# The first mixer's transposes, norms and output projection in another order

## The chip, the cores and the metric

The kernel runs on one core of one Trainium2 chip. The time is the device time of one execution in microseconds (us). Before the change it is 2455.3 us, the median of 3 runs (2453.57 to 2457.45).

## What is computed

256 tokens of width 1024 in float32 go through two blocks of two layers each. A layer of the first block, where the change lies, is a mixer and a gated feed-forward part:

```python
h = _rms_norm(x, attn_norm[l]) @ w_in[l]      # latent q, latent kv, rope key, differential q, k, v, grouped q, k, v
q_a  = (_rms_norm(h_cq) @ mla_w_uq[l])        # 6 latent heads, q and k normed and rotated
kv_a = (_rms_norm(h_ckv) @ mla_w_ukv[l])
o_a = softmax(q_a k_a) v_a
o_b = rms_norm((softmax(q1 k1) - lam * softmax(q2 k2)) v_b) * (1 - lambda_init)   # 4 differential heads
o_c = softmax(q_c k_c) v_c                    # 6 grouped heads on 2 key heads, rotated along two axes
x = x + concat(o_a, o_b, o_c) @ w_o[l]
x = x + (silu(xn @ gate) * (xn @ up)) @ w_down[l]
```

The second block (two other mixers, a dense and a mixture-of-experts feed-forward part) is not touched.

## The kernel before

**Weights.** Every float32 product is made of three: operands are split into a rounded part (hi) and the rest (lo), and `mm3` (lines 484 to 486) issues hi x hi, hi x lo and lo x hi. Weights come as a stream of halves of 128 x 1024, loaded by SP's queue into a ring of 8, cast by ACT (`w_hi`, line 420) and subtracted by DVE or, for the halves in `pool_halves` (the grouped chunks and eight of the ten halves of the output projection), by POOL (`w_lo`, line 426) into rings of 4. Each `half_step` makes PE use one half while ACT and DVE or POOL prepare the one three ahead.

**Units.** Activations that serve as an operand are transposed by PE in a unit (`unit`, line 673): up to four transposes into one bank (line 686), ACT copies hi (lines 691, 694), DVE subtracts lo (lines 699, 702). With `lag=1` PE waits until all units so far have their lo part; with `lag=2` one may be open.

**Ahead of the attention.** `first_layer` computes w_in's columns in chunks of two to four halves (`chunk`, `gemm_cols`): latent q, latent kv, differential q (2), differential k (3), then the products of the normed latents (`latent_rows`, query with three halves, key/value with two), then differential v (4). Each is evacuated by ACT and DVE (lines 994, 999, 1029, 1031). Beside the halves stand callbacks: beside chunk 2 the squares, three transposed units of the latents (`latent_blocks`) and a transposed gain (`gain_column`), beside chunk 3 the norm and rotation of the differential queries in three parts (`rotate`: squares and their sums, rotation, scaling), then their two units (`diff_blocks`); beside the query product the rotation of the keys, beside chunk 4 their units.

**The attention.** `attention` (line 709) is a pipeline over 20 maps (8 differential, 6 latent, 6 grouped), written out for each engine in program order; each engine has its own in-order queue, and semaphores alone tie them. In step s PE computes map s's scores; DVE takes their maximum (lines 780, 782), ACT the exponentials (line 792). PE transposes the probabilities of map s-2 (line 807), ACT copies them (line 733); PE multiplies those of map s-3 with the values (line 829), and DVE scales and writes the output (lines 835 to 846). Then comes `aside`, the filler `fill(step)` (line 1269), and behind it `units(step)` (line 1228):

- the filler holds PE's halves of the grouped chunks (`column_halves`) in steps 0 to 11 and, from step 15, one half of the output projection a step (`out_half`, 12 products of 512 columns into banks 4 to 7), the last two behind the loop; and DVE's norms and rotations of the latent heads (steps 0 to 5, lines 1098 to 1122), of the grouped queries (7 to 9) and keys (11, 12), and the norm of the differential outputs (`diff_norm`, lines 1157 to 1171, steps 11 and 12);
- units: the latent heads' in steps 6 to 11, the grouped ones in 12 and 13, behind them two units of the differential outputs, and from step 15 on, every second step, those of the other outputs. All those up to step 13 have `lag=1`.

DVE's part of a unit stands in its queue behind DVE's filler of the same step, PE's behind PE's.

Of the kernel before, what the change touches and what calls it, by code (L numbers as in the profile page):

```python
# [242 lines left out]
def build(nc, A):  # L243
    ctx = ExitStack()
    with ctx:
# [463 lines left out]
        def attention(E, maps, aside, act_copies=False, units=None, lag=1):  # L709
# [28 lines left out]
            if E.kind == "pe" and "made" not in maps[0]:  # L738

                e.wait_ge(qk_lo, E.qk.at())  # L740

                wait(e, acc_act, values)
                wait(e, acc_dve, values)
            for step in range(M + lag + 1):
# [69 lines left out]
                if 0 <= m < M:  # L814
# [17 lines left out]
                    if E.kind == "dve":  # L832
# [43 lines left out]
        def first_layer(E, l):  # L876
# [80 lines left out]
            def latent_blocks():  # L957


                if E.kind == "pe":  # L960
                    e.wait_ge(tp_lo, E.tp.at())
                    e.wait_ge(acc_act, E.acc.at())
                    e.wait_ge(acc_dve, E.acc.at())
                places = [(pair_of(b_cq), 0, 2), (pair_of(b_cq + 2, 1), 2, 1),
                          ((x_hi[:, KD:KD + nk, :], x_lo[:, KD:KD + nk, :]), nq, nk)]
                for dst, j, n in places:
                    g = CG_Q + j
                    unit(E, 2 + E.qk.n % 2, dst, [blk(H, C_CQ + (j + i) * P) for i in range(n)],
                         gains=colg[:, l, g:g + n], lag=2)

            def diff_blocks(c, b0):

                if E.kind == "pe":
                    e.wait_ge(qk_src, E.qks.at())
                for j in range(0, DH, 2):
                    unit(E, 2 + E.qk.n % 2, pair_of(b0 + j), [blk(H, c + (j + i) * P) for i in range(2)], lag=2)
# [69 lines left out]
            def beside_dk(hx):  # L1046
                if hx < 3:
                    rotate(hx, C_DQ, F_DQ, at_q)

            def beside_uq(hx):  # L1050
                rotate(hx, C_DK, F_DK, at_k)

            def beside_dv(hx):
                if hx == 2:
                    if E.kind == "pe":

                        e.wait_ge(acc_act, E.acc.at())
                        e.wait_ge(acc_dve, E.acc.at())
                    diff_blocks(C_DK, DH)
# [6 lines left out]
            chunk(2, beside_dq)  # L1066
            chunk(3, beside_dk)
# [4 lines left out]
            latent_rows(nk, MH * (MNOPE + MV) // 2, 0, (x_hi[:, KD:KD + nk, :], x_lo[:, KD:KD + nk, :]), KV, at_l + 2,  # L1072
                        nothing)
            chunk(4, beside_dv)

# [81 lines left out]
            def diff_norm(part):  # L1157

                x = O[:, :, MH * MV:MH * MV + DH * DV].rearrange("p t (h d) -> p t h d", h=DH)
                y = sc_mla[:, 0:TB * DH * DV]  # L1160
                if part == 0:
                    if E.kind == "dve":
                        drain_dve(E)
                        head_squares(E, x, DH, DV, 0, y)
                        mean_ready(E, 0, TB * DH, DV)
                    rsqrt(E, 0, TB * DH)
                elif E.kind == "dve":
                    need_rs(E)
                    e.tensor_tensor(x, x, scales(0, DH, DV), ALU.mult).then_inc(qk_src, 1)
# [58 lines left out]
            def units(step, ask=False):  # L1228
# [4 lines left out]
                if 6 <= step < 6 + MH:  # L1233
# [6 lines left out]
                    bk = 6 if step < 8 else 4 + step % 2  # L1240
                    unit(E, bk, pair_of(place(2 * h), 2, MQK), [blk(QA, h * MQK, MQK), blk(KA, h * MQK, MQK)], w=MQK)
                    ready[h] = E.qk.at()
                if step == 12 or step == 13:
# [3 lines left out]
                    unit(E, 4 + step % 2, pair_of(b_gq + j), [blk(H, C_GQ + (j + i) * P) for i in range(2)])  # L1247
# [47 lines left out]
            for h in range(DH):  # L1295
                for c in range(2):
                    o = MH * MV + h * DV
                    maps.append(dict(q=(h, c * 64, c * 64 + 64), k=(DH + h, c * 64, c * 64 + 64),
                                     scale=DQ ** -0.5, width=DV, minus=c == 1, ready=lambda n=E.qk.at(): n,
# [15 lines left out]
            for n in (8, 9):  # L1315
                out_half(n)
# [1292 lines left out]
```

## Time and profile before

| what | value |
|---|---|
| median of 3 runs | 2455.3 us |
| profiled execution | 2458.2 us |
| its span on the core | 2456.3 us |
| PE busy | 2310.7 us (94%) |
| DVE busy | 1733.9 us (71%) |
| ACT busy | 1460.9 us (59%) |
| POOL busy | 238.4 us (10%) |
| mean granted clock of TensorE | 0.968 |

The profile is of one execution. A clock of 1.00 is TensorE's full 2.4 GHz, 0.50 is 1.2 GHz; a mean between them is a share of time at each. The mixer of layer 0 lies between some 24 and 226 us of the span, that of layer 1 between some 430 and 625.

### The profile page before, as it was taken

The numbers are of one execution on the slowest core, as the hardware profiler recorded it, in microseconds if no ns is written. First come the engines' busy times: TensorE is split into PE (matmuls) and PEld (weight loads), VectorE is DVE, ScalarE is ACT, GpSimd is POOL, SyncE is SP. The second block draws the span as 40 slices with busy tenths as digits, with TensorE's granted clock in tenths as the row PEclk, the third lists the DMA queues.
The fourth block names the chain that finished last, engine by engine and source line by source line (L and its number), as shares of the span: only waits on it lengthen the run. The fifth ranks groups of instructions, "written<-read, shape, count | busy, mean of one in ns | idle before, by whom it ended". The sixth has DMA issues, their size and how long they took to land.

```text
span 2456.3 us, 31647 instructions
## 1 busy us (share of the span) xinstructions
PE 2310.7 (94%) x11904; PEld 1964.2 (80%) x11904; DVE 1733.9 (71%) x2370; ACT 1460.9 (59%) x2105; POOL 238.4 (10%) x140
## 2 busy tenths in 40 slices
PE   5889999888999899899899979999999999999997
PEld 5777887777788799788789868888888888888885
DVE  5864555773555544655653669989899999999998
ACT  4444444444444456444445557777777777777776
POOL 0422000142000232100215000000000000000000
PEclk9979999998999999999999989999999999999998
DMA  7313554521555544455463449999999999999996
GB/s 251 123 41 133 194 189 156 186 81 56 176 189 188 179 138 128 159 194 188 145 204 127 131 172 357 354 357 357 353 361 355 360 350 363 343 370 343 368 343 238
DMA packets 156989, 570.92 MB, mean 232 GB/s; under 512 B 18528, under 2 KB 18880, under 8 KB 156192
## 3 DMA queue, kind: packets, MB, share of 16 engines
q1 hardware_dynamic: 153744, 555.58, 64.6%
q0 software_dynamic: 3088, 13.27, 1.5%
q8 instruction: 97, 1.59, 0.2%
q14 instruction: 60, 0.49, 0.1%
HBM read 567.72 MB, written 1.05 MB: 232 GB/s over the span
## 4 chain that ended last, share of the span: by engine, by line
PE 86%; DVE 8%; ACT 2%; DMA 1%; issue 1%; POOL 1%; SPq 0%; DVEq 0%; POOLq 0%; ACTq 0%
PE bank L484 24%; PE bank L486 23%; PE bank L485 23%; PE bank L1729 3%; PE bank L1730 2%; PE bank L1731 2%; PE bank L829 2%; PE bank L1385 2%; PE bank L2199 1%; PE bank L807 1%; DVE w_lo L426 1%; PE bank L2220 1%; DMA arena<-in_bgate 1%; PE bank L686 1%; DVE X L1624 1%
## 5 line engine op out<-in xcount | busy, mean ns | idle before, releaser
L426 DVE TENSOR_TENSOR w_lo<-raw,w_hi 128x1024 fp32r<-128x1024 f32 x986 | 1192.2, 1227 | 320.1 <-ACT w_hi L420 292.2
L420 ACT CAST w_hi<-raw 128x1024 fp32r<-128x1024 f32 x1055 | 1101.4, 1051 | 364.7 <-PE bank L486 306.9
L484 PE MATMUL bank<-w_hi,x_hi 128*128 128x512 f32 (+2 forms) x2592 | 1024.5, 395 | 28.3 <-POOL w_lo L426 6.0
L486 PE MATMUL bank<-w_hi,x_lo 128*128 128x512 f32 (+2 forms) x2592 | 1004.2, 387 | 0.0
L485 PE MATMUL bank<-w_lo,x_hi 128*128 128x512 f32 (+2 forms) x2592 | 1002.7, 387 | 0.0
L484 PEld LDWEIGHTS bank<-w_hi,x_hi 128*128 128x128 f32 x2592 | 493.3, 190 | 123.4 <-POOL w_lo L426 9.5
L486 PEld LDWEIGHTS bank<-w_hi,x_lo 128*128 128x128 f32 x2592 | 491.8, 190 | 98.8
L485 PEld LDWEIGHTS bank<-w_lo,x_hi 128*128 128x128 f32 x2592 | 493.4, 190 | 89.8
L426 POOL TENSOR_TENSOR w_lo<-raw,w_hi 128x1024 fp32r<-128x1024 f32 x69 | 166.9, 2426 | 387.4 <-ACT w_hi L420 387.2
L1606 POOL TENSOR_TENSOR small<-small 128x1 f32<-128x1 f32 x10 | 8.6, 862 | 1353.9 <-ACT small L1602 1353.9
L1729 PE MATMUL bank<-x_hi,w_hi 128*128 128x256 f32 x384 | 111.6, 291 | 0.0
L1730 PE MATMUL bank<-x_lo,w_hi 128*128 128x256 f32 x384 | 109.1, 284 | 0.0
L1731 PE MATMUL bank<-x_hi,w_lo 128*128 128x256 f32 x384 | 109.1, 284 | 0.0
L1391 ACT CAST x_hi<-bank 128x256 fp32r<-128x256 f32 x112 | 41.9, 374 | 81.8 <-PE bank L2199 43.5
L829 PE MATMUL bank<-arena,PT 128*128 128x64 f32 (+1 forms) x576 | 81.3, 289 | 6.6 <-DVE O L846 6.0
L829 PEld LDWEIGHTS bank<-arena,PT 128*128 128x128 f32 x576 | 77.8, 210 | 8.1 <-issue 8.1
L733 ACT COPY PT<-bank 128x512 f32<-128x512 f32 x56 | 32.8, 586 | 77.6 <-PE bank L807 77.6
L1410 ACT ACTIVATE arena<-bank 128x256 f32<-128x256 f32 x134 | 50.4, 384 | 44.0 <-PE bank L486 44.0
L1730 PEld LDWEIGHTS bank<-x_lo,w_hi 128*128 128x128 f32 x384 | 74.2, 193 | 0.0
L1729 PEld LDWEIGHTS bank<-x_hi,w_hi 128*128 128x128 f32 x384 | 74.2, 193 | 0.1
L1731 PEld LDWEIGHTS bank<-x_hi,w_lo 128*128 128x128 f32 x384 | 74.0, 193 | 0.0
L792 ACT ACTIVATE PP<-bank,small 128x256 f32<-128x256 f32 x80 | 37.3, 473 | 56.2 <-DVE small L782 56.0
(226 smaller groups left out, 1869.1 us busy)
## 6 DMA issues: line engine op xcount, KB each, us to landing
raw<-in_stream SPq DMA_DIRECT2D x1055, 512.0 KB, 5.7
tab<-in_lngb POOLq DMA_DIRECT2D x5, 1024.0 KB, 7.9
arena<-in_rpb POOLq DMA_DIRECT2D x16, 256.0 KB, 7.4
tab<-in_rowv POOLq DMA_DIRECT2D x2, 640.0 KB, 8.1
X<-in_x SPq DMA_DIRECT2D x1, 1024.0 KB, 5.2
out_y<-X SPq DMA_DIRECT2D x2, 512.0 KB, 2.6
tab<-in_ropec POOLq DMA_DIRECT2D x2, 448.0 KB, 5.1
tab<-in_ropes POOLq DMA_DIRECT2D x2, 448.0 KB, 6.2
```

Source lines behind the costliest of these rows:

```text
L420: nc.scalar.copy(w_hi[:, s % SPLIT, :], raw[:, slot, :]).then_inc(hi_done, 1)
L426: e.tensor_tensor(w_lo[:, s % SPLIT, :], raw[:, s % RAW, :], w_hi[:, s % SPLIT, :].bitcast(F32), ALU.subtract).then_inc(done, 1)
L484: pe.matmul(out, xh, wh, start=first, stop=False)
L485: pe.matmul(out, xh, wl, start=False, stop=False)
L486: return pe.matmul(out, xl, wh, start=False, stop=last)
L829: i = e.matmul(ob[:, tb * w:(tb + 1) * w], PT[:, m % 2, kb, tb * P:(tb + 1) * P], a["v"](kb), start=kb == 0, stop=kb == TB - 1)
L1385: i = e.transpose(tr[f][:, tb * P:(tb + 1) * P], HH[:, tb, f * P:(f + 1) * P], ident[:, :])
L1391: i = nc.scalar.copy(hT_hi[:, :, 0:T], both)
L1410: i = nc.scalar.activation(SIL[:, tb, :], bank[b0 + tb][:, 0:FC], ACT.Silu, scale=rsx[:, tb:tb + 1] if scaled else 1.0)
L1729: e.matmul(out, wh, xh, start=first, stop=False, skip_group_check=True)
L1730: e.matmul(out, wh, xl, start=False, stop=False, skip_group_check=True)
L1731: return e.matmul(out, wl, xh, start=False, stop=last, skip_group_check=True)
```

## The change

Units now stand ahead of the step's filler on every engine, except those of steps 15, 17, 19 and 21, which stay behind it. All units up to step 13 have `lag=2`, and the first two take two banks. The norm of the differential outputs is made in two halves of two heads: the first in steps 6 and 7, the second in 10 and 11; its first unit moves from step 13 to 11. The grouped key chunk's second half moves from step 10 to 9. The output projection starts in step 14, and one half instead of two is left behind the loop. Ahead of the attention, the three latent units stand behind halves 1, 2 and 3 of chunk 2, the gain column beside chunk 3; the rotation of the differential keys is spread over the query product's second half and both halves of the key/value product; the four differential units stand beside and behind chunk 4, a query and a key unit in turn. The two waits in front of the attention's first step go; the one for the evacuation stands ahead of the first filler half.

```diff
--- before.py
+++ after.py
@@ attention
-            if E.kind == "pe" and "made" not in maps[0]:
-                e.wait_ge(qk_lo, E.qk.at())
-                wait(e, acc_act, values)
-                wait(e, acc_dve, values)
...
+                if units and not units(step, True):
+                    units(step)
                 aside(step)
-                if units:
-                    if E.kind == "pe" and lag <= step < M + lag and units(step, True):
+                if units and units(step, True):
+                    if E.kind == "pe" and step < M + lag:
                         e.wait_ge(*copied(step - lag))
                     units(step)
@@ ahead of the attention
-            def latent_blocks():
-                if E.kind == "pe":
+            def latent_blocks(which):
+                if E.kind == "pe" and which == 0:
...
-                for dst, j, n in places:
-                    g = CG_Q + j
-                    unit(E, 2 + E.qk.n % 2, dst, ..., gains=colg[:, l, g:g + n], lag=2)
+                dst, j, n = places[which]
+                g = CG_Q + j
+                unit(E, 2 + which % 2, dst, ..., gains=colg[:, l, g:g + n], lag=2)
-            def diff_blocks(c, b0):
+            def diff_blocks(j, q):
+                c, b0 = (C_DQ, 0) if q else (C_DK, DH)
                 if E.kind == "pe":
-                    e.wait_ge(qk_src, E.qks.at())
-                for j in range(0, DH, 2):
-                    unit(E, 2 + E.qk.n % 2, pair_of(b0 + j), ..., lag=2)
+                    e.wait_ge(qk_src, diff_made[q])
+                unit(E, 3 if q else 2, pair_of(b0 + j), ..., lag=2)
+                diff_ready[j // 2] = E.qk.at()
             def beside_dq(hx):
                 if hx == 0:
                     latent_squares()
-                if hx == 1:
-                    latent_blocks()
-                if hx == 2:
-                    gain_column()
+                else:
+                    latent_blocks(hx - 1)
             def beside_dk(hx):
+                if hx == 0:
+                    gain_column()
                 if hx < 3:
                     rotate(hx, C_DQ, F_DQ, at_q)
+                if hx == 2:
+                    diff_made[1] = E.qks.at()
             def beside_uq(hx):
-                rotate(hx, C_DK, F_DK, at_k)
+                if hx == 1:
+                    rotate(0, C_DK, F_DK, at_k)
+            def beside_ukv(hx):
+                rotate(hx + 1, C_DK, F_DK, at_k)
+                if hx == 1:
+                    diff_made[0] = E.qks.at()
             def beside_dv(hx):
-                if hx == 2:
-                    if E.kind == "pe":
-                        e.wait_ge(acc_act, E.acc.at())
-                        e.wait_ge(acc_dve, E.acc.at())
-                    diff_blocks(C_DK, DH)
+                if hx == 1 and E.kind == "pe":
+                    e.wait_ge(acc_act, E.acc.at())
+                    e.wait_ge(acc_dve, E.acc.at())
+                if hx:
+                    diff_blocks(hx // 3 * 2, hx % 2)
...
             chunk(3, beside_dk)
-            diff_blocks(C_DQ, 0)
             latent_rows(nq, ..., at_l, beside_uq)
...
-            latent_rows(nk, ..., at_l + 2, nothing)
+            latent_rows(nk, ..., at_l + 2, beside_ukv)
             chunk(4, beside_dv)
+            diff_blocks(2, 0)
@@ diff_norm
-            def diff_norm(part):
-                x = O[:, :, MH * MV:MH * MV + DH * DV]...
+            def diff_norm(h0, part):
+                n = DH // 2
+                at = h0 * TB
+                x = O[:, :, MH * MV + h0 * DV:MH * MV + (h0 + n) * DV]...
@@ units
-                    bk = 6 if step < 8 else 4 + step % 2
-                    unit(E, bk, pair_of(place(2 * h), 2, MQK), ..., w=MQK)
+                    bk = 6 + step % 2 if step < 8 else 4 + step % 2
+                    unit(E, bk, pair_of(place(2 * h), 2, MQK), ..., w=MQK, lag=2)
                     ready[h] = E.qk.at()
+                if step == 11:
+                    if E.kind in ("act", "dve"):
+                        e.wait_ge(og_done, l + 1)
+                    if E.kind == "pe":
+                        e.wait_ge(qk_src, made["diff01"])
+                        e.wait_ge(acc_act, E.acc.at())
+                        e.wait_ge(acc_dve, E.acc.at())
+                    out_unit(6, 3, 2, 2 * DH, scale=og_col[:, 0:1], lag=2)
                 if step == 12 or step == 13:
...
-                    unit(E, 4 + step % 2, pair_of(b_gq + j), ...)
+                    unit(E, 4 + step % 2, pair_of(b_gq + j), ..., lag=2)
                 if step == 13:
-                    if E.kind in ("act", "dve"):
-                        e.wait_ge(og_done, l + 1)
                     if E.kind == "pe":
-                        e.wait_ge(qk_src, made["diff"])
-                        e.wait_ge(acc_act, E.acc.at())
-                        e.wait_ge(acc_dve, E.acc.at())
-                    for j in range(2):
-                        out_unit(6 + j, 3 + 2 * j, 2, 2 * DH, scale=og_col[:, 0:1])
+                        e.wait_ge(qk_src, made["diff23"])
+                    out_unit(7, 5, 2, 2 * DH, scale=og_col[:, 0:1], lag=2)
@@ fill
                 if step in (0, 2, 4, 6, 7):
+                    if step == 0 and E.kind == "pe":
+                        wait(e, acc_act, E.acc.at())
+                        wait(e, acc_dve, E.acc.at())
                     next(gq, None)
-                if step in (8, 10, 11):
+                if step in (8, 9, 10):
                     if step == 8 and E.kind == "pe":
-                        e.wait_ge(qk_lo, E.qk.at())
+                        e.wait_ge(qk_lo, ready[1])
                     next(gkv, None)
-                if step >= 15:
-                    out_half(step - 15)
+                if step >= 14:
+                    out_half(step - 14)
...
+                if step == 6:
+                    diff_norm(0, 0)
+                if step == 7:
+                    diff_norm(0, 1)
+                    made["diff01"] = E.qks.at()
...
+                if step == 10:
+                    diff_norm(DH // 2, 0)
                 if step == 11:
-                    diff_norm(0)
+                    diff_norm(DH // 2, 1)
+                    made["diff23"] = E.qks.at()
                     grouped(0, C_GK, GKV, F_GK, at_g + TB * GH)
                 if step == 12:
-                    diff_norm(1)
-                    made["diff"] = E.qks.at()
...
             out_unit(2, 9, 1, 0)
-            for n in (8, 9):
-                out_half(n)
+            out_half(9)
```

## Rows read from the trace of the kernel before

**Rows 1.** The page: busy time by engine, and the chain that ended last.

```profile
PE 2310.7 (94%) x11904; PEld 1964.2 (80%) x11904; DVE 1733.9 (71%) x2370; ACT 1460.9 (59%) x2105; POOL 238.4 (10%) x140
...
PE 86%; DVE 8%; ACT 2%; DMA 1%; issue 1%; POOL 1%; SPq 0%; DVEq 0%; POOLq 0%; ACTq 0%
```

**Rows 2.** Busy us by stretch, layer 0: PE, PEld, DVE, ACT, POOL; clock.

```profile
66.70:84.20 17.50, 11.73 (x68) 11.17 (x68) 16.70 (x20) 9.58 (x13) 2.90 (x1) 0.90 0.42 136
...
99.90:124.40 24.50, 20.10 (x122) 17.84 (x123) 23.58 (x43) 11.44 (x32) 11.47 (x4) 0.89 0.26 85
...
124.40:169.80 45.40, 34.22 (x231) 32.17 (x230) 33.31 (x73) 20.57 (x53) 12.46 (x6) 0.80 0.11 36
...
169.80:182.60 12.80, 12.80 (x53) 11.26 (x52) 3.19 (x9) 4.64 (x12) 2.38 (x1) 0.58 0.01 1
...
182.60:226.40 43.80, 39.66 (x222) 32.56 (x220) 15.71 (x35) 17.91 (x36) 9.53 (x4) 1.00 0.35 111
```

**Rows 3.** The same view, second layer.

```profile
522.70:568.30 45.60, 33.19 (x227) 31.35 (x226) 33.27 (x73) 20.54 (x53) 12.46 (x6) 0.84 0.12 37
...
568.30:581.50 13.20, 13.20 (x53) 11.56 (x52) 3.19 (x9) 4.64 (x12) 2.37 (x1) 0.56 0.02 4
```

**Rows 4.** PE timeline ahead of the attention: start, us, [idle before, releaser].

```profile
49.54 0.65 PE L686 MATMUL bank<-ident,arena 128*128 128x128 f32 x4 [1.63 <-DVE qk_l L702]
...
68.66 1.09 PE L686 MATMUL bank<-ident,arena 128*128 128x128 f32 x8 [1.99 <-DVE arena L942]
...
71.65 0.61 PE L484 MATMUL bank<-w_hi,qk_t 128*128 128x288 f32 x1 [1.90 <-DVE qk_l L699]
...
84.25 0.47 PE L484 MATMUL bank<-w_hi,x_hi 128*128 128x512 f32 x1 [1.96 <-DVE arena L1031]
...
98.94 0.35 PE L484 MATMUL bank<-qk_t 64*128 64x256 f32 x1 [1.05 <-DVE arena L999]
```

**Rows 5.** DVE's timeline ahead of the attention and at its first step.

```profile
69.66 0.74 DVE L999 TENSOR_SCALAR arena<-bank,small 128x512 f32<-128x512 f32 x1
...
86.33 1.13 DVE L1031 TENSOR_SCALAR arena<-bank,small 128x384 f32<-128x384 f32 x2
...
99.92 0.69 DVE L780 TENSOR_REDUCE small<-bank 128x2 f32<-128x512 f32 x1 [1.23 <-PE bank L486]
```

**Rows 6.** DVE's timeline in the attention's steps 3 to 13.

```profile
112.58 3.22 DVE L1108 TENSOR_TENSOR arena<-arena,small 128x1152 f32<-128x1152 f32 x1
...
128.81 0.69 DVE L699 SCALAR_TENSOR_TENSOR qk_l<-bank,qk_t 96x512 fp32r<-96x512 f32 x1 [2.25 <-ACT qk_t L691]
...
137.49 3.34 DVE L665 TENSOR_TENSOR arena<-arena,tab 128x192 f32<-128x192 f32 x4
...
150.91 0.69 DVE L699 SCALAR_TENSOR_TENSOR qk_l<-bank,qk_t 96x512 fp32r<-96x512 f32 x1 [2.98 <-ACT qk_t L691]
...
153.24 1.23 DVE L650 TENSOR_TENSOR arena<-O 128x1024 f32<-128x1024 f32 x1
...
165.06 0.69 DVE L699 SCALAR_TENSOR_TENSOR qk_l<-bank,qk_t 128x512 fp32r<-128x512 f32 x1 [1.18 <-ACT qk_t L691]
...
170.62 0.75 DVE L699 SCALAR_TENSOR_TENSOR x_lo<-bank,small,x_hi 128x512 fp32r<-128x512 f32 x1 [1.99 <-ACT x_hi L691]
```

**Rows 7.** POOL's timeline, two of its weight splits in the attention.

```profile
112.24 2.35 POOL L426 TENSOR_TENSOR w_lo<-raw,w_hi 128x1024 fp32r<-128x1024 f32 x1
...
137.53 2.55 POOL L426 TENSOR_TENSOR w_lo<-raw,w_hi 128x1024 fp32r<-128x1024 f32 x1 [1.11 <-ACT w_hi L420]
```

**Rows 8.** PE's timeline, steps 14, 15, 20 and 21 of the attention.

```profile
169.79 0.58 PE L484 MATMUL bank<-qk_t 64*128 64x256 f32 x1
...
178.06 0.77 PE L484 MATMUL bank<-w_hi,x_hi 128*128 128x512 f32 x1
...
206.85 0.48 PE L484 MATMUL bank<-w_hi,x_hi 128*128 128x512 f32 x1
...
209.71 0.60 PE L807 MATMUL bank<-ident,PP 128*128 128x128 f32 x4
```

More of the change, by code:

```diff
@@ L965, in latent_blocks @@
                           ((x_hi[:, KD:KD + nk, :], x_lo[:, KD:KD + nk, :]), nq, nk)]
-                for dst, j, n in places:
-                    g = CG_Q + j
-                    unit(E, 2 + E.qk.n % 2, dst, [blk(H, C_CQ + (j + i) * P) for i in range(n)],
-                         gains=colg[:, l, g:g + n], lag=2)
-            def diff_blocks(c, b0):
+                dst, j, n = places[which]
+                g = CG_Q + j
+                unit(E, 2 + which % 2, dst, [blk(H, C_CQ + (j + i) * P) for i in range(n)],
+                     gains=colg[:, l, g:g + n], lag=2)
+            def diff_blocks(j, q):
+                c, b0 = (C_DQ, 0) if q else (C_DK, DH)
                 if E.kind == "pe":
-                    e.wait_ge(qk_src, E.qks.at())
-                for j in range(0, DH, 2):
-                    unit(E, 2 + E.qk.n % 2, pair_of(b0 + j), [blk(H, c + (j + i) * P) for i in range(2)], lag=2)
+                    e.wait_ge(qk_src, diff_made[q])
+                unit(E, 3 if q else 2, pair_of(b0 + j), [blk(H, c + (j + i) * P) for i in range(2)], lag=2)
+                diff_ready[j // 2] = E.qk.at()
             def gain_column():
@@ L1072, in first_layer @@
             latent_rows(nk, MH * (MNOPE + MV) // 2, 0, (x_hi[:, KD:KD + nk, :], x_lo[:, KD:KD + nk, :]), KV, at_l + 2,
-                        nothing)
+                        beside_ukv)
             chunk(4, beside_dv)
+            diff_blocks(2, 0)
             def place(n):
@@ L1163, in diff_norm @@
                         drain_dve(E)
-                        head_squares(E, x, DH, DV, 0, y)
-                        mean_ready(E, 0, TB * DH, DV)
-                    rsqrt(E, 0, TB * DH)
+                        head_squares(E, x, n, DV, at, y)
+                        mean_ready(E, at, TB * n, DV)
+                    rsqrt(E, at, TB * n)
                 elif E.kind == "dve":
                     need_rs(E)
-                    e.tensor_tensor(x, x, scales(0, DH, DV), ALU.mult).then_inc(qk_src, 1)
+                    e.tensor_tensor(x, x, scales(at, n, DV), ALU.mult).then_inc(qk_src, 1)
                 if part == 1:
@@ L1239, in units @@
                             e.wait_ge(acc_dve, E.acc.at())
-                    bk = 6 if step < 8 else 4 + step % 2
-                    unit(E, bk, pair_of(place(2 * h), 2, MQK), [blk(QA, h * MQK, MQK), blk(KA, h * MQK, MQK)], w=MQK)
+                    bk = 6 + step % 2 if step < 8 else 4 + step % 2
+                    unit(E, bk, pair_of(place(2 * h), 2, MQK), [blk(QA, h * MQK, MQK), blk(KA, h * MQK, MQK)], w=MQK,
+                         lag=2)
                     ready[h] = E.qk.at()
+                if step == 11:
[6 more added lines that the diff above has]
+                    out_unit(6, 3, 2, 2 * DH, scale=og_col[:, 0:1], lag=2)
                 if step == 12 or step == 13:
@@ L1246, in units @@
                         e.wait_ge(qk_src, made["gq" if j == 0 else "gk"])
-                    unit(E, 4 + step % 2, pair_of(b_gq + j), [blk(H, C_GQ + (j + i) * P) for i in range(2)])
+                    unit(E, 4 + step % 2, pair_of(b_gq + j), [blk(H, C_GQ + (j + i) * P) for i in range(2)], lag=2)
                     ready[MH] = E.qk.at()
                 if step == 13:
-                    if E.kind in ("act", "dve"):
-                        e.wait_ge(og_done, l + 1)
                     if E.kind == "pe":
-                        e.wait_ge(qk_src, made["diff"])
-                        e.wait_ge(acc_act, E.acc.at())
-                        e.wait_ge(acc_dve, E.acc.at())
-                    for j in range(2):
-                        out_unit(6 + j, 3 + 2 * j, 2, 2 * DH, scale=og_col[:, 0:1])
+                        e.wait_ge(qk_src, made["diff23"])
+                    out_unit(7, 5, 2, 2 * DH, scale=og_col[:, 0:1], lag=2)
                 if step == 15:
@@ L1298, in first_layer @@
                     maps.append(dict(q=(h, c * 64, c * 64 + 64), k=(DH + h, c * 64, c * 64 + 64),
-                                     scale=DQ ** -0.5, width=DV, minus=c == 1, ready=lambda n=E.qk.at(): n,
+                                     scale=DQ ** -0.5, width=DV, minus=c == 1, ready=lambda h=h: diff_ready[h // 2],
                                      v=lambda kb, h=h: H[:, kb, C_DV + h * DV:C_DV + (h + 1) * DV],
```

7 lines of the change are left out of this document (4 added, 3 removed).

## The prediction

> **What bounds the kernel now.** I read the page first, for the shares of the span; then the busy time in stretches of the mixer; then the timelines of PE and DVE, for who waits for whom. On the page PE is busy 94% of the span and carries 86% of the chain that ended last, DVE 8% [rows 1]. The change touches only the first block's mixer, twice (layers 0 and 1), so the averages do not price it. The stretches do. Between 124.4 and 169.8 us (steps 6 to 13 of the attention) PE is busy 34.22 of 45.40 us at a mean clock of 0.80; in steps 14 and 15 it is busy all 12.80 us, but at 0.58; after that 39.66 of 43.80 at 1.00 [rows 2]. Layer 1 repeats it within a few tenths: 33.19 of 45.60, then 13.20 at 0.56 [rows 3]. So everything below is worked out on layer 0 and doubled. Steps 0 to 5 are DVE's: 23.58 of 24.50 us busy [rows 2], so whatever moves step 0 on DVE moves the rest with it. DMA's share in these stretches is 0.42, 0.26, 0.11, 0.01 and 0.35: SP's weight loads, whose order stays, are no bound here, and the later stages move up with whatever the mixer gives.
>
> **Ahead of the attention.** Three stalls of PE are addressed.
>
> Latent units, one behind each half of the differential-query chunk instead of three in a row: the wait of 1.63 us for the first unit's lo part goes [rows 4]. What is late next is DVE: it must evacuate this chunk and rotate while PE runs the next, and the third unit's lo now stands ahead of that evacuation. Of the 1.6 I pass on 1.1.
>
> Differential-query blocks out of the gap behind the key chunk: today PE waits 1.99, transposes 1.09, waits 1.90 and starts the query product at 71.65 [rows 4]. Without them it still waits for DVE's evacuation of the chunk, which ends at 69.66 + 0.74 = 70.40 [rows 5]: 1.25 gained, not 5.
>
> Key rotation spread over the query and the key/value products: DVE evacuates the query product before two of the three parts instead of behind all, so the wait of 1.96 ahead of the values' chunk goes [rows 4]. In exchange the first differential unit, behind that chunk's second half, waits for the key/value product's evacuation. That ended at 86.33 + 1.13 = 87.46 [rows 5] with no rotation ahead of it; now two parts of the rotation stand there. Replaying DVE's queue with today's durations puts it at about 87.8, against a PE ready at 85.4: a new wait of 2.4. The four units cost as many transposes as before, in smaller groups: 0.1. Less time at the slow clock behind the old gap: I take 0.8 of gain.
>
> At the seam, step 0's scores no longer wait 1.05 for the chunk's evacuation [rows 4], but on DVE that evacuation and two lo parts now stand ahead of step 0's maximum, which started at 99.92 [rows 5]. It comes 3.3 us behind the chunk's end, against 2.0 now: +1.3.
>
> Sum: -1.1 - 1.25 - 1.96 + 2.4 + 0.1 - 0.8 + 1.3 = **-1.3 us**. Bounds 0 (the new wait eats it all) and -3 (it does not occur). It passes whole through steps 0 to 5.
>
> **Steps 6 to 13.** Units now stand ahead of the filler. Today DVE runs the filler while PE, behind its own filler, has yet to transpose; where DVE has no filler it waits: 2.25 in step 6, 2.98 in step 10, then 1.18 and twice about 1.99 in step 13, where four units follow each other one round trip at a time [rows 6]. Sum 10.4. What stays of them: 0.45 in steps 6 and 10, and 1.2 in step 13, where the two output units take other banks and may run one ahead: 2.1.
>
> Added: in steps 7, 8, 9, 11 and 12 DVE now waits in front of its filler, and behind that filler is the next step's maximum, for which ACT's exponentials and PE wait. No row shows this wait in these places. Bounds: 0.5, if DVE's own reciprocal and output work covers it, and 2.98, the longest wait for the same releaser [rows 6]. Nearest is the 1.18 at 165.06, where ACT came straight from the exponentials to the unit, as it will now [rows 6]; part of that lies under the output evacuation of the heads with the minus sign. I take 0.85: 5 x 0.85 = 4.25. The norm in two halves: a 1024-element operation is 1.23 [rows 6], a 512-element one 0.69 [rows 5], so 2 x 0.69 - 1.23 = 0.15 for each of three, and one more small one: 0.6. The second power on POOL is needed only a step later, and covered.
>
> So the last lo comes 10.4 - 2.1 - 4.25 - 0.6 = 3.45 earlier. Step 14's scores, started at 169.79 [rows 8], ran 1.6 ahead of the end of that last lo (170.62 + 0.75 = 171.37 [rows 6]); now they run 0.75 ahead, one unit: 3.45 - 0.85 = 2.6 gained.
>
> Against it stands POOL. L1108 took 3.22 us beside POOL's weight split of 112.24, where 1152 elements at L650's rate are 1.4; the four L665 took 3.34 beside the split of 137.53, where they are some 1.2 [rows 6, 7]: about 2.0 lost each time. The Trainium skill, "SBUF — State Buffer", section "Who interferes with whom", says that a DVE instruction with two SBUF inputs and a GpSimd one that reads SBUF exclude each other, the later blocking until the first is done; the trace agrees. The unit ahead moves ACT's split in step 6, and the key chunk's half moves from step 10 to 9, so two of POOL's splits may newly meet fillers. Bounds 0 and 4.0; I take 1.2, since reductions, units' lo parts and evacuations fill much of that time. Net **-1.4 us**.
>
> **The output projection a step earlier.** A half with the clock up is 209.71 - 206.85 = 2.86 us [rows 8]. It leaves the tail: **-2.9 us**, since the steps after, of PE's, keep one half each, and the waits for the last units are the same. It does not fall into idle time: PE is busy all of steps 14 and 15. But it is at the low level of 1.2 GHz: two steps without a half took 178.06 - 169.79 = 8.3 us, 4.1 each [rows 8]. Now: step 14's attention work slow, 4.1; its half between 2.86 and 5.7, I take 3.9; then step 15 at full clock, 2.1 + 2.9 + 0.6 for its unit: 13.6, against 12.80 [rows 2]. **+0.8 us** (bounds -2.3 and +4.6, below).
>
> **Sum**: -1.3 - 1.4 + 0.8 - 2.9 = -4.8 a layer, -9.6 for both. The profiled execution took 2458.2 us for a span of 2456.3; it would take 2448.6. The median of the runs is 2.9 under it, so **2445.7 us**. Other edits (the waits in front of the attention dropped, bank 7 beside 6, the gain column a chunk later) have no queue behind them that is late.
>
> **Rivals.**
>
> A, the forecast: its own range 2440 to 2451, chance 0.48.
>
> B, the clock comes up with step 14: both steps at full clock are 2 x (2.1 + 2.9) + 0.5 = 10.5, 2.3 under now, 3.1 a layer better than A: **2439.5**. For it: between 169.8 and 182.6 PE was busy throughout and still at 0.58, and the clock rose only behind the first dense half [rows 2, 8]. The page "TensorE: Matmul & The Clock Gate" of the Trainium skill, section "Part 4: PE-mode transpose", says that transposes do not count as PE work for the clock; with a dense half in step 14 that rule favours B. Against: the half itself still starts slow. 0.18.
>
> C, POOL's splits hit fully: 4.0 instead of 1.2, so -2.0 a layer: **2451.3**, within 0.2%. 0.14.
>
> D, slower: DVE's new waits in front of the fillers are as long as today's longest. PE transposes only behind the output product, which waits for DVE's last output, so both could wait in turn. At 2.6 each: 5 x (2.6 - 0.85) = +8.75, +3.95 a layer: **2463.2**. It decides from 2.3 us a wait. Against it: ACT has nothing between exponentials and unit. 0.08.
>
> E, the earlier half does not do what it is moved for: it runs slow to its end and step 15's attention too, 4.1 + 5.7 + 4.1 + 2.9 + 0.6 = 17.4, 3.8 over A's 13.6: -1.0 a layer: **2453.3**. 0.12.
>
> **How the numbers follow.** A measurement of this kernel can tell about 0.2%, 4.9 us, from no change. Faster by more: nearly all of A, B, a sixth of C: 0.70. Within: C, E and A's edge: 0.22. Slower by more: D, 0.08. The range 2437 to 2455 takes in B, C and E and leaves out D and B's far side.
>
> **What would show it.** Right: the seam's maximum on DVE 1 to 2 us earlier; PE's 1.63 and 1.96 gone and a wait of some 2.4 in the values' chunk; waits of DVE for ACT's unit of 0.5 to 1.2 in steps 7 to 13 and none of 2 or more; step 14's scores some 3 us earlier; a half between steps 14 and 15. Wrong: steps 6 to 13 no shorter than 45 us (C, D), or the stretch from step 14 to 16 near 10.5 (B) or 17 (E).

## The result and the profile after

| kernel | median | runs | profiled execution | its span |
|---|---|---|---|---|
| before, measured beside it | 2456.44 us | 10 | 2458.2 us | 2456.3 us |
| after | 2463.47 us | 10 | 2463.08 us | 2461.2 us |

The ratio is 1.0027, with an interval of 1.0017 to 1.0037: slower by 6.6 us by the ratio, by 7.0 by the medians. The forecast was 9.6 us faster, and the time lies above its range. Two executions at a low granted clock, one of the kernel after (2931.45 us, clock 0.744) and one of e8_again below (3731.3 us, clock 0.572, the only profiled one of that run, whose trace is therefore not read), stand in the medians and not in the ratios.

The page of the kernel after, to be read against [rows 1]: PE has the same work, DVE 10 us more, and the chain names DVE and "issue" one per cent more each.

```profile
span 2461.2 us, 31662 instructions
...
PE 2310.2 (94%) x11904; PEld 1960.2 (80%) x11904; DVE 1744.1 (71%) x2378; ACT 1457.0 (59%) x2105; POOL 245.1 (10%) x142
...
PE 85%; DVE 9%; ACT 2%; issue 2%; DMA 1%; POOL 1%; SPq 0%; DVEq 0%; POOLq 0%; ACTq 0%
```

That says only that a wait was added. Where it stands is read from stages. I cut every kernel's mixer at the same events, by their starts on the timelines: the first latent unit on PE; step 0's and step 6's maximum on DVE; the scores of steps 14 and 16 on PE; the first transpose behind the mixer. For the kernel after, layer 0, the view of stretches (PE, PEld, DVE, ACT and POOL busy, granted clock, DMA's share, GB/s) has one row for each stage:

```profile
45.49:103.55 58.06, 46.20 (x216) 39.10 (x215) 40.45 (x45) 22.93 (x32) 17.29 (x6) 0.88 0.44 147
103.55:128.02 24.47, 18.59 (x124) 15.87 (x123) 23.56 (x45) 11.32 (x32) 11.47 (x4) 0.99 0.24 80
128.02:173.06 45.04, 33.95 (x228) 31.20 (x227) 36.95 (x78) 20.22 (x54) 14.14 (x7) 0.84 0.11 36
173.06:186.34 13.28, 13.28 (x65) 11.24 (x65) 2.94 (x9) 4.88 (x12) 3.85 (x2) 0.79 0.14 41
186.34:227.44 41.10, 36.95 (x210) 30.31 (x209) 15.72 (x35) 16.84 (x35) 8.07 (x4) 1.00 0.35 113
```

The lengths of these stages in all kernels, in us, layer 0 / layer 1. The kernels from e1_rs on are those of the experiments, below. All lengths are of one execution each, and the first stage moves by itself by up to 1.5: e5_half has the code of before there, but 52.70 against 51.19 in layer 1, where PE's wait ahead of the values' chunk is 2.00 in the one and 0.66 in the other.

| kernel | ahead of step 0 | steps 0-5 | 6-13 | 14-15 | tail | sum |
|---|---|---|---|---|---|---|
| before | 52.83 / 51.19 | 24.49 / 24.50 | 45.38 / 45.65 | 12.85 / 13.24 | 43.78 / 43.81 | 179.33 / 178.39 |
| after | 58.06 / 58.08 | 24.47 / 24.49 | 45.04 / 45.03 | 13.28 / 14.85 | 41.10 / 41.05 | 181.95 / 183.50 |
| e1_rs | 55.39 / 54.30 | 24.47 / 24.49 | 45.05 / 45.04 | 13.44 / 13.49 | 41.04 / 41.06 | 179.39 / 178.38 |
| e6_dvesplit | 50.57 / 50.56 | 24.50 / 24.48 | 45.05 / 45.07 | 14.26 / 13.57 | 41.07 / 41.08 | 175.45 / 174.76 |
| e2_rot | 50.00 / 51.68 | 24.46 / 24.46 | 45.04 / 45.04 | 13.84 / 13.92 | 41.08 / 41.06 | 174.42 / 176.16 |
| e4_pre | 58.23 / 59.89 | 24.48 / 25.56 | 43.37 / 44.14 | 13.29 / 12.65 | 43.78 / 43.82 | 183.15 / 186.06 |
| e3_attn | 51.72 / 50.13 | 24.50 / 24.47 | 45.03 / 45.02 | 13.15 / 13.75 | 41.06 / 41.04 | 175.46 / 174.41 |
| e5_half | 52.71 / 52.70 | 24.49 / 24.49 | 44.85 / 44.86 | 14.32 / 14.32 | 41.04 / 41.03 | 177.41 / 177.40 |
| e8_seam | 50.34 / 48.83 | 24.52 / 24.50 | 45.05 / 45.07 | 14.25 / 14.35 | 41.08 / 41.08 | 175.24 / 173.83 |
| e9_order | 48.86 / 48.84 | 24.49 / 24.50 | 45.59 / 44.85 | 14.53 / 14.29 | 41.08 / 41.08 | 174.55 / 173.57 |

Of the kernel after one stage is long: ahead of step 0, +5.2 and +6.9. The tail gave its 2.7, and steps 6 to 13, for which most of the change is written, moved by 0.3 and 0.6. The sums of both layers differ by 7.7 us, the two profiled spans by 4.9: the part ahead of layer 0's first latent unit is 1.6 shorter, the part behind layer 1's tail 1.5 shorter and the part between the mixers 0.3 longer. No edit stands there, and the cause was not looked for.

**The long stage.** PE's timeline of the kernel after, with the query product, the first halves of the values' chunk, and its first unit:

```profile
67.87 0.58 PE L484 MATMUL bank<-w_hi,qk_t 128*128 128x288 f32 x1 [4.50 <-DVE arena L996]
...
79.11 0.39 PE L484 MATMUL bank<-w_hi,x_hi 128*128 128x512 f32 x1
...
82.51 0.50 PE L484 MATMUL bank<-w_hi,x_hi 128*128 128x512 f32 x1 [0.47 <-DVE w_lo L426]
...
91.62 1.09 PE L686 MATMUL bank<-ident,arena 128*128 128x128 f32 x4 [6.09 <-issue]
92.36 0.78 PE L484 MATMUL bank<-w_hi,x_hi 128*128 128x512 f32 x1
...
97.23 0.60 PE L686 MATMUL bank<-ident,arena 128*128 128x128 f32 x4
...
100.42 1.03 PE L686 MATMUL bank<-ident,arena 128*128 128x128 f32 x8
```

The query product starts 22.4 us behind the stage's begin, where it was 24.6 (71.65, [rows 4], less 47.09), and the values' chunk 33.6 instead of 37.2. So 3.5 us have been gained by 79.11. Then PE stands still for 6.09 ahead of the first differential unit, and the half behind it takes 4.87 (92.36 to 97.23) where the next takes 2.83 (97.59 to 100.42). The releaser is given as "issue": the profile doesn't name it. By the program it is the evacuation of the key/value product on DVE (L1028), which must end before PE may transpose. DVE's timeline shows it and what stood ahead of it:

```profile
72.25 1.22 DVE L426 TENSOR_TENSOR w_lo<-raw,w_hi 128x1024 fp32r<-128x1024 f32 x1 [3.51 <-ACT w_hi L420]
...
81.23 1.23 DVE L426 TENSOR_TENSOR w_lo<-raw,w_hi 128x1024 fp32r<-128x1024 f32 x1 [3.02 <-ACT w_hi L420]
...
86.08 3.25 DVE L426 TENSOR_TENSOR w_lo<-raw,w_hi 128x1024 fp32r<-128x1024 f32 x1
...
90.39 1.13 DVE L1028 TENSOR_SCALAR arena<-bank,small 128x384 f32<-128x384 f32 x2
...
103.55 0.68 DVE L774 TENSOR_REDUCE small<-bank 128x2 f32<-128x512 f32 x1
```

The evacuation ends at 91.52, and PE goes on at 91.62. Ahead of it DVE waited 3.02 for a cast of ACT's, and one weight split took 3.25 instead of 1.2. ACT's timeline has the cause of the first, POOL's of both:

```profile
75.15 0.89 ACT L1026 ACTIVATE arena<-bank,small 128x288 f32<-128x288 f32 x2 [0.49 <-PE bank L486]
80.14 2.00 ACT L420 CAST w_hi<-raw 128x1024 fp32r<-128x1024 f32 x2 [4.11 <-POOL small L541]
```

```profile
76.31 3.81 POOL L541 TENSOR_TENSOR small<-small 128x16 f32<-128x16 f32 x1 [13.75 <-DVE small L655]
85.06 3.19 POOL L426 TENSOR_TENSOR w_lo<-raw,w_hi 128x1024 fp32r<-128x1024 f32 x1 [4.95 <-ACT w_hi L420]
```

L541 is the power that makes the scales of a norm. The one of 76.31 belongs to the differential keys; ACT needs nothing of it. But `latent_rows` opens on ACT with `need_rs`, which waits until all scales asked for so far are made, and ahead of the key/value product the keys' scales are among them. They were so before the change too, and the count that is waited for is the same. What changed is when they are asked for: beside the query product's first half before, beside its second half now. POOL's and ACT's timelines of the kernel before, at the same place:

```profile
75.55 2.90 POOL L541 TENSOR_TENSOR small<-small 128x16 f32<-128x16 f32 x1 [10.21 <-DVE small L655]
```

```profile
78.16 0.89 ACT L1029 ACTIVATE arena<-bank,small 128x288 f32<-128x288 f32 x2 [0.48 <-PE bank L486]
78.94 1.05 ACT L420 CAST w_hi<-raw 128x1024 fp32r<-128x1024 f32 x1
```

There the power began 3.9 us behind the query product's start (71.65, [rows 4]) and was over at 78.45, while ACT was busy until 79.05 with the evacuation that stands ahead of its wait. So ACT didn't stand, by 0.6 us. In the kernel after, the power begins 8.4 us behind that start (67.87); ACT has done the same evacuation at 76.04 and stands 4.11 us, until 76.31 + 3.81 = 80.12, for scales that it doesn't use. Its casts come late, DVE's splits behind them, and POOL's first split of the grouped weights (85.06 to 88.25) lies beside DVE's of 86.08. **A wait for everything asked for so far grew, because a request that it had always included was moved later**; neither the wait's line nor its count is in the diff. This is the theory that the experiments test. Its rivals are that the new wait is the one forecast (rotation in front of the evacuation), only longer, and that the loss lies in the attention (rival D).

### The profile page after: what moved, and what is told of

It reads as the page before. It is cut to its first block, busy times and chain, and to the rows that moved or that the text cites. A ratio compares the mean times of both kernels' runs of the same rounds, so it can differ in the third digit from the quotient of the medians.

```text
span 2461.2 us, 31662 instructions
## 1 busy us (share of the span) xinstructions
PE 2310.2 (94%) x11904; PEld 1960.2 (80%) x11904; DVE 1744.1 (71%) x2378; ACT 1457.0 (59%) x2105; POOL 245.1 (10%) x142
## 3 DMA queue, kind: packets, MB, share of 16 engines
HBM read 567.72 MB, written 1.05 MB: 231 GB/s over the span
## 4 chain that ended last, share of the span: by engine, by line
PE 85%; DVE 9%; ACT 2%; issue 2%; DMA 1%; POOL 1%; SPq 0%; DVEq 0%; POOLq 0%; ACTq 0%
PE bank L484 24%; PE bank L486 23%; PE bank L485 23%; PE bank L1750 3%; PE bank L1751 2%; PE bank L1752 2%; PE bank L823 2%; PE bank L1406 2%; PE bank L2220 1%; PE bank L801 1%; DVE w_lo L426 1%; PE bank L2241 1%; DMA arena<-in_bgate 1%; DVE small L774 1%; DVE X L1645 1%
## 5 line engine op out<-in xcount | busy, mean ns | idle before, releaser
L823 PEld LDWEIGHTS bank<-arena,PT 128*128 128x128 f32 x576 | 72.8, 198 | 23.6 <-issue 23.6
```

The costliest lines, as they stand in the source:

```text
L823: i = e.matmul(ob[:, tb * w:(tb + 1) * w], PT[:, m % 2, kb, tb * P:(tb + 1) * P], a["v"](kb), start=kb == 0, stop=kb == TB - 1)
```

## The experiments

The times of before are of runs on the same chip beside each kernel; they moved between 2456.4 and 2457.0.

**e1_rs**: ACT waits for the latents' scales alone. Edit to the kernel after:

```diff
                 rsqrt(E, at_l, 4)
+                latent_rs[0] = E.rs.at()
...
                 if E.kind == "act":
-                    need_rs(E)
+                    e.wait_ge(rs_ready, latent_rs[0])
```

> The changed kernel, but ACT waits ahead of each latent product for the latents' own scales (the count right behind their request) instead of for every scale asked for so far. Theory (the wait): in the changed kernel the keys' first rotation part stands ahead of the key/value product, so ACT's wait includes its scales; ACT stood 4.1 us (80.14), DVE 3.0 behind it, a POOL split then met a DVE split (3.25 instead of 1.2). Expected: ACT's 4.1 and DVE's 3.0 gone in both layers, PE's wait in the values' chunk 6.1 down to 3 or less, step 0's maximum 3 to 6.5 us earlier a layer; 6 to 13 us under the changed kernel, so between 2450 and 2457 where the kernel before is 2456 and the changed one 2463. Rival (load): DVE's moved work alone makes the gap; then the wait moves, and the time stays within 2 us of the changed kernel.

Measured: 2457.42 us, ratio to before 1.0005 (0.9996 to 1.0014), 6.0 less than the kernel after. In the trace ACT's 4.11 and DVE's 3.02 are gone. PE's timeline, then DVE's and POOL's, at the same unit:

```profile
89.40 1.08 PE L686 MATMUL bank<-ident,arena 128*128 128x128 f32 x4 [3.40 <-issue]
```

```profile
84.85 3.39 DVE L938 TENSOR_TENSOR arena<-PP,small 128x1024 f32<-128x1024 f32 x1
88.17 1.13 DVE L1031 TENSOR_SCALAR arena<-bank,small 128x384 f32<-128x384 f32 x2
```

```profile
84.50 2.66 POOL L426 TENSOR_TENSOR w_lo<-raw,w_hi 128x1024 fp32r<-128x1024 f32 x1 [3.65 <-ACT w_hi L420]
```

The edit loosens the wait ahead of both latent products, but ahead of the query product ACT didn't stand for POOL in the kernel after. So the wait ahead of the key/value product cost 6.0 us of the execution. That is the small end of the 6 to 13 expected, and PE's wait, 3.40, is above the 3 that was. The kernel is still no faster than before: the last part of the rotation now meets POOL's split, 3.39 for 1.2, and the evacuation is late again, by less.

**e2_rot**: the keys' rotation wholly beside the query product, as before the change; all else as after.

```diff
             def beside_uq(hx):
-                if hx == 1:
-                    rotate(0, C_DK, F_DK, at_k)
-
-            def beside_ukv(hx):
-                rotate(hx + 1, C_DK, F_DK, at_k)
-                if hx == 1:
+                rotate(hx, C_DK, F_DK, at_k)
+                if hx == 2:
                     diff_made[0] = E.qks.at()
```

> The changed kernel with the keys' rotation back beside the three halves of the query product, as before. Theory (the wait): its scales are then asked for a half earlier, and nothing but splits stands ahead of the key/value evacuation: no wait of 4.1 on ACT, none over 1 us in the values' chunk, but the 1.96 for the query product's evacuation is back. Expected 2449 to 2453 (attention's 2.6 a layer kept, 0 to 1.5 a layer gained ahead of it). Rival (load): the four units in the values' chunk and the seam cost by themselves; then 2458 or more.

Measured: 2448.22 us, ratio 0.9964 (0.9950 to 0.9977), 15.2 under the kernel after and 0.8 under the range expected. The stage ahead is 50.00 and 51.68. PE's timeline has the wait that the spreading was to remove, smaller than the 1.96 of [rows 4], and no wait ahead of the first differential unit:

```profile
80.31 0.47 PE L484 MATMUL bank<-w_hi,x_hi 128*128 128x512 f32 x1 [1.16 <-ACT arena L1026]
...
85.85 0.60 PE L686 MATMUL bank<-ident,arena 128*128 128x128 f32 x4
```

**e3_attn and e4_pre**: the change in two, each a version of the kernel before. e3_attn has all edits inside and behind the attention (units ahead of the filler, the norm in halves, the moved key half, the half in step 14, no waits in front of step 0), e4_pre all those ahead of it.

```diff
+                if units and not units(step, True):
+                    units(step)
                 aside(step)
...
-                if step >= 15:
-                    out_half(step - 15)
+                if step >= 14:
+                    out_half(step - 14)
```

> Only the attention's part of the change (units ahead of the filler, norm in halves, output projection from step 14); everything ahead of the attention as before. From the changed kernel's trace: steps 6 to 13 0.35 shorter, steps 14 and 15 0.45 longer, the tail 2.7 shorter, 2.6 a layer: 2451 where the kernel before is 2456 (2449 to 2453). Rival: the attention's part loses by itself (new DVE waits ahead of fillers, and POOL's splits): 2456 or more.

> Only the part ahead of the attention; the attention as before, its two waits in front among it. Both theories: about 5.2 us a layer lost there, less 0 to 1 a layer from the seam, which keeps the old order of waits: 2464 to 2468 where the kernel before is 2456. If it is 2459 or less, the two parts hurt each other and the sum is not of parts.

Measured: e3_attn 2449.21 us, ratio 0.9974 (0.9963 to 0.9985), −7.2; e4_pre 2470.46 us, ratio 1.0057 (1.0044 to 1.0071), +14.1. They add up: 14.1 − 7.2 = 6.9, where the whole change is +7.0. e4_pre is 2.5 above the range expected. The whole loss is ahead of the attention, +5.4 and +8.7 in the table (one other stage of e4_pre, steps 0 to 5 of layer 1, is 1.1 longer than in all others, which was not looked into), and in e4_pre ACT's timeline has the same wait, now 4.95:

```profile
80.89 1.99 ACT L420 CAST w_hi<-raw 128x1024 fp32r<-128x1024 f32 x2 [4.95 <-POOL small L541]
```

**e5_half**: the kernel before with the output projection from step 14, nothing else.

```diff
-                if step >= 15:
-                    out_half(step - 15)
+                if step >= 14:
+                    out_half(step - 14)
...
-            for n in (8, 9):
-                out_half(n)
+            out_half(9)
```

> The kernel before with one edit: the output projection starts in step 14 instead of 15, so one half instead of two is left behind the loop. The attention's part of the change as a whole measured 7.2 us (3.6 a layer). Theory: the half alone gives the 2.7 of the tail, against 0.4 more in steps 14 and 15, 2.3 a layer: about 2452 where the kernel before is 2456.4; the rest of the 3.6 belongs to units ahead of the filler and the norm in halves. Rival (clock): the half brings the clock up as well, and the units ahead give nothing: 2449 to 2450.

Measured: 2450.47 us, ratio 0.9971 (0.9959 to 0.9983), −6.5, so by the medians these few lines give nearly all of e3_attn's 7.2. In the profile the tail gives 2.7 and 2.8, and steps 14 and 15 take 1.5 and 1.1 of it back. From step 0 on the stages of both layers sum to 4.3 less than before here, and to 5.7 less in e3_attn. So the time lies near the rival's 2449 to 2450, and the stages near the theory's 2.3 a layer; the profiled execution took 2453.98 us, 3.5 above the median, and which of the two holds is open. The stretches of steps 6 to 13 and of 14 and 15:

```profile
122.59:167.44 44.85, 32.84 (x225) 30.78 (x225) 33.77 (x73) 20.44 (x53) 12.45 (x6) 0.82 0.12 37
167.44:181.76 14.32, 14.32 (x66) 12.02 (x65) 3.19 (x9) 5.58 (x13) 3.84 (x2) 0.73 0.12 38
```

**e6_dvesplit**: e1_rs, and the first half of the grouped weights is split by DVE instead of POOL.

```diff
-        own |= set(range(a - H_GROUPED, a + H_O - 2))
+        own |= set(range(a - H_GROUPED + 1, a + H_O - 2))
```

> The kernel e1_rs (ACT waits for the latents' scales alone), and the lo part of the first grouped half, which POOL made at 84.5 beside the keys' last rotation part on DVE (3.39 us instead of 1.22), is made by DVE instead. Theory (collision): the last rotation part takes 1.2 us again, the key/value evacuation comes 2.2 earlier, PE's wait of 3.4 in the values' chunk falls to about 1.2, and the slow clock behind it (a half of 5.2 us instead of 2.7) may go too: 2 to 5 us a layer, 2447 to 2453 where e1_rs is 2457.4. Rival (load): DVE is as full as before, the wait stays near 3 and the time within 2 us of 2457.

Measured: 2449.63 us, ratio 0.9968 (0.9956 to 0.9980), 7.8 under e1_rs. DVE's timeline, then PE's, then the stretch around the first unit (columns as above):

```profile
85.29 1.22 DVE L938 TENSOR_TENSOR arena<-PP,small 128x1024 f32<-128x1024 f32 x1
86.43 1.14 DVE L1031 TENSOR_SCALAR arena<-bank,small 128x384 f32<-128x384 f32 x2
```

```profile
87.67 0.63 PE L686 MATMUL bank<-ident,arena 128*128 128x128 f32 x4 [2.47 <-issue]
```

```profile
84.00:100.00 16.00, 12.74 (x74) 10.51 (x73) 11.58 (x16) 6.57 (x12) 4.77 (x2) 1.00 0.54 174
```

The rotation's last part takes 1.22 again, and PE's wait is 2.47: the prediction had said 2.4, the expectation of this run 1.2. The clock stays at 1.00 through that wait, where in e1_rs and in the kernel after it fell. Of the 4.8 us by which this stage is shorter in layer 0, 2.2 are the operation (3.39 − 1.22), and 2.7 the stretch from the first unit to the second, 3.23 us here and 5.90 in e1_rs, at half the clock. Whether the longer wait alone set the clock there was not tried. With ACT's wait and POOL's collision gone, spreading the rotation still gains nothing over leaving it where it was: e2_rot took 2448.22.

**e8_seam**: from e2_rot, both query units behind the values' second half and both key units behind the third, none behind the chunk. So only the chunk's own evacuation stands ahead of step 0's maximum.

```diff
-                if hx:
-                    diff_blocks(hx // 3 * 2, hx % 2)
+                if hx == 1 or hx == 2:
+                    diff_blocks(0, hx % 2)
+                    diff_blocks(2, hx % 2)
...
             chunk(4, beside_dv)
-            diff_blocks(2, 0)
```

> The kernel e2_rot (keys' rotation beside the query product), and both differential query units behind the second half of the values' chunk, both key units behind the third, none behind the last. Theory (seam): DVE has only the chunk's evacuation between its end and step 0's maximum, which comes 2.0 us behind that end instead of 3.2; 1.2 a layer, 2445 to 2446.5 where e2_rot is 2448.2. Rival: DVE's later work or the clock takes it back: 2447.5 or more.

> The kernel e8_seam a second time, beside e9_order on the same chip: 2444 to 2448, the measure against which e9_order is read.

Measured: 2445.93 us, ratio 0.9955 (0.9942 to 0.9969), and in the second set of runs 2445.70, 0.9951 (0.9937 to 0.9964). Two to three us under e2_rot, which is about what the intervals can tell. The last product of the chunk ends here where the scores of step 0 begin, at 95.86, and the maximum starts 1.0 behind that, where it was 3.1 in the kernel after; the transposes of two units, 0.8, now stand ahead of that end instead. The seam on DVE:

```profile
95.97 0.75 DVE L996 TENSOR_SCALAR arena<-bank,small 128x512 f32<-128x512 f32 x1 [1.27 <-PE bank L486]
96.86 0.69 DVE L774 TENSOR_REDUCE small<-bank 128x2 f32<-128x512 f32 x1
```

**e9_order**: e8_seam with the attention of before (units behind the filler with `lag=1`, one norm in steps 11 and 12, the key half in step 10), but with the projection from step 14 and without the waits in front of step 0.

```diff
-                if units and not units(step, True):
-                    units(step)
                 aside(step)
-                if units and units(step, True):
-                    if E.kind == "pe" and step < M + lag:
+                if units:
+                    if E.kind == "pe" and lag <= step < M + lag and units(step, True):
```

> The part ahead of the attention of e8_seam and the earlier output projection of e5_half, with the attention otherwise as in the kernel before: units behind the filler, lag 1 up to step 13, norm of the differential outputs in one piece. Theory (DVE's queue): with units ahead, steps 6 to 13 take 45.0 us in every kernel so far, whatever the clock; behind the filler they took 43.4 to 45.6, the clock deciding. So the order gives nothing: 2443 to 2447, within 2 us of e8_seam (2445.9) or under it. Rival (the order gains): e8_seam's order is worth the 1.4 us a layer that was forecast; then 2448 to 2450.

Measured: 2444.72 us, ratio 0.9950 (0.9936 to 0.9964): the best kernel of the study, 12.1 us under before and 18.8 under after. Beside e8_again it can't be told from e8_seam, and from step 0 on the stages of both layers sum to 0.5 more than e8_seam's. So putting the units ahead of the filler and cutting the norm in two, the larger part of the diff, is worth nothing that was measured here.

## Why the prediction was wrong

By its own terms, us a layer:

| term | forecast | layer 0 / layer 1 |
|---|---|---|
| ahead of step 0 | −1.3 | +5.2 / +6.9 |
| steps 0 to 5 | 0 | 0.0 / 0.0 |
| steps 6 to 13 | −1.4 | −0.3 / −0.6 |
| steps 14 and 15 | +0.8 | +0.4 / +1.6 |
| tail | −2.9 | −2.7 / −2.8 |
| sum | −4.8 | +2.6 / +5.1 |

**The step that failed** is "Replaying DVE's queue with today's durations puts it at about 87.8, against a PE ready at 85.4: a new wait of 2.4". The wait was found, its place and the order of the operations in it too, but only DVE's queue was replayed. Two things were left out. ACT's queue: the keys' scales are asked for later, ACT's `need_rs` waits for them, and ACT feeds the splits that DVE's queue begins with. And POOL's: the prediction asked in the attention what a split of POOL's newly meets, and not here, though the keys' rotation moves to where the grouped weights begin to be split. In place of the 2.4 the runs show 6.56 us of waiting in the chunk; e1_rs, without ACT's wait, 3.40; and e6_dvesplit, without POOL's split either, 2.47.

The stage's sum in layer 0, worked out as the forecast did: the way to the values' chunk gave 3.5 (forecast 1.1 + 1.25 + 1.96 = 4.3); the chunk's waits cost 0.47 + 6.09 = 6.6 (2.4); PE's own time in the chunk rose by 1.1, from 13.64 (98.94 − 1.05 − 84.25, [rows 4]) to 14.75 (100.42 − 79.11 − 6.56), where the forecast had −0.8 + 0.1 for less slow clock; the seam cost 1.1, since the maximum comes 3.13 behind the chunk's end instead of 2.03 (+1.3). −3.54 + 6.56 + 1.11 + 1.10 = +5.23. So two terms were fair (the way to the chunk and the seam), the wait was 4.2 too small, and the clock had the wrong sign: the slow clock behind the longer wait (below) cost more than the forecast's 0.8 of gain.

**Steps 6 to 13.** The waits of DVE for ACT's unit were forecast at 6.35 in all (2.1 that stay, 4.25 new). The view of waits for this stretch (us in total, times, longest) gives

```profile
DVE qk_l L699 <- ACT qk_t L691: 6.6, 8, 1.2
```

so the mechanism was right to a few tenths, and rival D, with 2.6 a wait, is out. What was too small is the price of POOL. DVE's idle time fell by 4.0 us (12.07 to 8.09), but it is busy 36.95 us here, where it was 33.31 [rows 2]. Small operations and a rotation stand beside its splits, first on DVE's timeline and then on POOL's:

```profile
132.67 1.51 DVE L655 TENSOR_SCALAR small<-small 128x4 f32<-128x4 f32 x1
...
144.38 3.36 DVE L665 TENSOR_TENSOR arena<-arena,tab 128x192 f32<-128x192 f32 x4
...
153.57 1.46 DVE L776 TENSOR_SCALAR small<-small 128x2 f32<-128x2 f32 x1
```

```profile
131.46 2.69 POOL L426 TENSOR_TENSOR w_lo<-raw,w_hi 128x1024 fp32r<-128x1024 f32 x1 [6.44 <-ACT w_hi L420]
...
152.21 2.79 POOL L426 TENSOR_TENSOR w_lo<-raw,w_hi 128x1024 fp32r<-128x1024 f32 x1 [4.95 <-ACT w_hi L420]
```

The same L776 takes 0.17 with POOL idle. The two new meetings are 1.34 and 1.29, 2.6 in all against 1.2 forecast, which is more than the 1.1 that is missing (−1.4 against −0.3); the other terms, within some tenths, were not parted. Whether the units ahead would gain without these meetings was not tried. All kernels with the units ahead take 45.02 to 45.07 here, though TensorE's mean clock in layer 0 ranges from 0.80 (e1_rs) to 0.90 (e6_dvesplit), with DVE busy 36.93 to 36.97; those with the units behind vary from 43.4 to 45.7. That suggests that in the new order DVE's chain bounds these steps. By the prediction's own sign, no shorter than 45 us, rival C came true here in part.

**Steps 14 and 15** took 13.28 in layer 0, 0.3 under A's 13.6, and 14.85 in layer 1, between A and E's 17.4; before they took 12.85 and 13.24. B is out: the clock's mean is 0.79 and 0.70, not 1. **The tail** came as forecast. The dropped waits in front of step 0, costed at nothing, were not tried alone: e3_attn's first stage is 1.1 shorter than before in both layers, which is within what that stage moves by itself.

**The rivals**: D had the right side for another reason, and that its 2463.2 stands so close to the 2463.47 measured is luck: the waits that it priced at 2.6 each are 1.2 at the longest. No rival stood for a new wait of ACT, nor for a stage ahead of the attention that loses; its bounds (0 to −3) let nothing above zero in, and that was the error behind the range. The bound "the new wait eats it all" was taken for the worst, while the wait's own price had been given as one number.

## What to carry to other kernels

When work is moved, replay every engine's queue from the moved instruction on, and look for waits on a running count that include it, whether it stands ahead of them newly or always did: they now end when it does, and no line of the diff says so. A consumer should wait for its own request's count, as in e1_rs. And of a large reordering, try the plainest part alone: here a few lines gave 6.5 us, and the reordering of the units nothing that was measured on top.

## What was not expected of the hardware

A weight split of POOL's holds up even the smallest operation of DVE: 4 elements a partition took 1.51 us (132.67), 2 elements 1.46 (153.57), instead of 0.17, each until 0.03 behind the modelled end of POOL's split (134.15 and 155.00). The Trainium skill, "SBUF — State Buffer", section "Who interferes with whom", says that the order of issue and not the shape decides who blocks, and that a `tensor_scalar` can take the pair of ports that both share, when its operands meet certain conditions. The trace agrees beside POOL's splits. Beside POOL's powers it doesn't: L776 took 0.17 at 159.97, within the L541 of 159.42 to 160.43, which reads SBUF too; why was not looked into. The forecast had priced only large operations, though the trace of the kernel before shows a small one held up. DVE's timeline, then POOL's:

```profile
104.38 0.92 DVE L782 TENSOR_SCALAR small<-small 128x2 f32<-128x2 f32 x1
```

```profile
102.88 2.39 POOL L426 TENSOR_TENSOR w_lo<-raw,w_hi 128x1024 fp32r<-128x1024 f32 x1 [3.66 <-ACT w_hi L420]
```

TensorE's clock was at its low level behind the two longest of PE's gaps ahead of the first differential unit, though the half that follows has the same products as the others. The stretch from the first unit to the second, of the same sixteen-odd instructions, in three kernels; the kernel after, behind 6.09 us of idle time:

```profile
91.62:97.23 5.61, 5.61 (x16) 4.52 (x17) 1.72 (x2) 1.53 (x2) 2.38 (x1) 0.54 0.66 215
```

e1_rs, behind 3.40:

```profile
89.40:95.30 5.90, 5.90 (x17) 4.74 (x17) 1.72 (x2) 1.53 (x2) 2.37 (x1) 0.51 0.53 178
```

e6_dvesplit, behind 2.47:

```profile
87.67:90.90 3.23, 3.23 (x16) 2.67 (x17) 2.76 (x3) 1.54 (x2) 0.95 (x1) 1.00 0.45 152
```

The first two are almost wholly at 1.2 GHz, the third at 2.4. What else differs between them was not parted. In these two cases the stretch took 2.4 and 2.7 us more than in the third, which the forecast, pricing the new wait by its length alone, had nowhere.
